# The first eight input-weight blocks loaded as float32 and cast on the chip, in a pooling and retention layer

## What is computed

```python
hn = rms_norm(h, norm_w)                 # norm_w scales the 1024 columns of hn
proj = hn @ w_in                         # w_in: 1024 x 6144 float32
u, gp, q, k, v, gr = split(proj, 6)      # 1024 columns each
pool_o = (trailing means of u over 2/4/8/16 - u) @ w_pool * pool_scale
q, k = rotary(q), rotary(k)
o = retention(q, k, v)                   # chunks of 128 rows, a state per head
ret = rms_norm(o) * ret_norm_w * silu(gr)
y = rms_norm(h + concat(pool_o * silu(gp), ret) @ w_out) * final_norm_w
```

## Time and profile before

| | us |
|---|---|
| median of 3 runs | 619.95 (616.08 to 620.24) |
| the profiled execution | 618.45 |
| its span, slowest core (5) | 616.9 |
| spans of the eight cores | 605.4 to 616.9 |
| PE busy | 570.6 (93%) |
| DVE busy | 414.6 (67%) |
| ACT busy | 266.0 (43%) |
| POOL busy | 112.5 (18%) |

### The profile page before, as it was taken

The page is one execution under the profiler, slowest core; times in us unless marked ns, Lnnn a source line. Parts: engine busy times, 40 slices in busy tenths (PEclk is TensorE's granted clock), DMA queues, the critical chain, the costliest instruction groups (busy, mean ns, idle before and its releaser), DMA issues.

```text
span 616.9 us, 13819 instructions; the slowest of 8 cores (605.4 to 616.9 us)
## 1 busy us (share of the span) xinstructions
PE 570.6 (93%) x4360; PEld 313.9 (51%) x4360; DVE 414.6 (67%) x1114; ACT 266.0 (43%) x831; POOL 112.5 (18%) x131
## 2 busy tenths in 40 slices
PE   0699995999699999999999999999999999899994
PEld 0244452588354646555565646464454655455651
DVE  3349997477888755856676785867767673866463
ACT  2345463553333443343345344353644534355331
POOL 6300001121010111110011122322413310330010
PEclk9999997999899999999999999999999999999998
DMA  8999999486723542544263355575775635454621
GB/s 139 212 168 181 168 172 165 83 112 113 129 73 108 133 126 60 117 103 108 72 114 120 49 171 131 182 159 118 209 137 177 166 102 142 101 152 88 123 69 38
DMA packets 90034, 78.52 MB, mean 127 GB/s; under 512 B 56254, under 2 KB 72814, under 8 KB 89948
## 3 DMA queue, kind: packets, MB, share of 16 engines
q1 hardware_dynamic: 74524, 60.09, 39.5%
q0 software_dynamic: 15440, 17.55, 20.3%
HBM read 64.57 MB, written 18.41 MB: 135 GB/s over the span
## 4 chain that ended last, share of the span: by engine, by line
PE 82%; DMA 9%; DVE 3%; POOL 2%; issue 1%; another core or an unknown queue 1%; SPq 0%; DVEq 0%; POOLq 0%; ACT 0%; ACTq 0%
PE pp L588 42%; PE pp L863 20%; PE pp L603 8%; DMA w_in_bf<-w_in 6%; PE pp L837 2%; DMA w_out_bf<-w_out 2%; PE pp L929 2%; PE pp L916 1%; PE pp L818 1%; PE pp L748 1%; PE pp L707 1%; PE pp L724 1%; PE pp L750 1%; DVE w_in_bf L507 1%
## 5 line engine op out<-in xcount | busy, mean ns | idle before, releaser
L588 PE MATMUL pp<-w_in_bf,hnTs 128*128 128x512 bf16 x1120 | 260.9, 384 | 19.7 <-DMA w_in_bf<-w_in 18.2
L588 PEld LDWEIGHTS pp<-w_in_bf,hnTs 128*128 128x128 bf16 x1120 | 105.4, 99 | 144.3 <-issue 32.5
L863 PE MATMUL pp<-w_out_bf,yT 128*128 128x512 bf16 x448 | 102.2, 383 | 0.3
L623 ACT ACTIVATE F<-pp,dec 128x128 f32<-128x128 f32 (+1 forms) x216 | 61.7, 369 | 59.2 <-PE pp L588 54.1
L863 PEld LDWEIGHTS pp<-w_out_bf,yT 128*128 128x128 bf16 x448 | 43.1, 99 | 53.2 <-issue 4.0
L526 POOL TENSOR_TENSOR rs_r<-rs_r,nh 128x4 f32<-128x4 f32 x32 | 35.5, 1111 | 169.9 <-DVE rs_r L523 169.6
L603 PE MATMUL pp<-hnTs,w_in_bf 128*128 128x128 bf16 x896 | 53.5, 219 | 0.0
L603 PEld LDWEIGHTS pp<-hnTs,w_in_bf 128*128 128x128 bf16 x896 | 51.0, 98 | 3.4 <-issue 0.9
L872 ACT ACTIVATE pp<-xr 128x512 f32<-128x512 f32 x30 | 18.0, 601 | 74.5 <-DVE xr L870 64.5
L910 POOL TENSOR_TENSOR scr<-vM,ident 16x512 bf16<-16x512 bf16 x32 | 35.3, 1102 | 79.4 <-PE pp L916 76.0
L786 DVE SCALAR_TENSOR_TENSOR ry<-pp,rs_r,G 128x128 bf16<-128x128 f32 x104 | 29.2, 343 | 19.6 <-POOL rs_r L526 19.3
(11 more groups left out here) (167 smaller groups left out, 767.0 us busy)
## 6 DMA issues: line engine op xcount, KB each, us to landing
w_in_bf<-w_in POOLq DMA_DIRECT2D x12, 1024.0 KB, 54.8
scr<-S_in SPq DMA_DIRECT2D x32, 256.0 KB, 3.5
Ss<-scr SPq DMA_DIRECT2D x32, 256.0 KB, 3.1
xr<-x SPq DMA_DIRECT2D x15, 512.0 KB, 3.8
y<-xr SPq DMA_DIRECT2D x15, 512.0 KB, 2.8
xA<-x SPq DMA_DIRECT2D x14, 512.0 KB, 4.4
w_out_bf<-w_out POOLq DMA_DIRECT2D x4, 1024.0 KB, 15.2
w_out_bf<-x SPq DMA_DIRECT2D x3, 512.0 KB, 7.4
```

The costliest lines, as they stand in the source:

```text
L588: r = e.matmul(bk(b)[:T, :], lhsT=h.ap[:, kc * T:(kc + 1) * T], rhs=w_in_bf[:, kc, c0:c0 + 512], start=(kc == 0), stop=(kc == 7))
L623: r = e.activation(out=Fa.ap[:T, i * 128:(i + 1) * 128], in_=bk(b)[:T, i * 128:(i + 1) * 128], func=AF.Copy, scale=dec[:T, dslot * 8 + h:d ...
L863: r = e.matmul(bk(b)[:T, :], lhsT=yap[:, kc * st:kc * st + T], rhs=w_out_bf[:, kc, nt * 512:(nt + 1) * 512], start=(kc == 0), stop=(kc == 15))
```

## The change

The first eight blocks no longer go through a casting DMA. SP loads them as float32 into the places of blocks 0 and 1 (loads 0, 2, 4 and 6) and 2 and 3 (loads 1, 3, 5 and 7), which together hold just one float32 block each. DVE, ACT and POOL then each cast a part of the eight 512-column rows of a block (3, 3 and 2) to bf16 in its own place and multiply it by the norm weight in the same operation. The first load is cut in two halves of 1 MB. Blocks 0 to 3 come last, as before by casting DMAs from POOL, when the eight are cast; DVE and ACT fold the norm weight into them, four rows each. So the turned tiles need no factor: A2 copies them out of PSUM with one ACT operation instead of eight on DVE, and `fold_w` is gone. The small loads at the start are put in line with the weight loads on SP's queue "w"; the loads of mask, band, ident and w_out stay on POOL, in a queue "p".

```diff
-WORD = [(10, 11, 6, 7), (8, 9, 4, 5), (2, 3, 0, 1)]
+WORD = (10, 11, 6, 7, 8, 9, 4, 5)
+WLATE = (0, 1, 2, 3)
+SHARE = (("dve", 3), ("act", 3), ("pool", 2))
...
-    def load_w(blk):
+    def wk(blk):
+        return ["win%d%s" % (blk, z) for z in ("dve", "act", "pool", "dvey", "acty", "pooly")]
+
+    def load_w(i, blk):
+        a = i % 2
+        st = w_in_bf[:, :, a * 1024:(a + 1) * 1024].bitcast(F32)
+        parts = 1 if i else 2
+        n = 8 // parts
+        for h in range(parts):
+            sk = [k + "xy"[z] for k in ("st%d" % a,) for z in ((0, 1) if parts == 1 else (h,))]
+            own = wk(2 * a) + wk(2 * a + 1) if i else []
+            ks = slice(h * n, (h + 1) * n)
+            dma("sp", st[:, ks, :], w_in_v[:, ks, blk * 512:(blk + 1) * 512], [], sk + own, (1 << 21) // parts,
+                "d_st%d%d" % (a, h), queue="w")
+            k0 = h * n
+            for z, (eng, m) in enumerate(SHARE if parts == 1 else (("dve", 2), ("act", 1), ("pool", 1))):
+                def f(e, eng=eng, k0=k0, m=m):
+                    r = None
+                    for kc in range(k0, k0 + m):
+                        w = w_in_bf[:, kc, blk * 512:(blk + 1) * 512]
+                        s = normw[:, kc:kc + 1]
+                        if eng == "act":
+                            r = e.activation(out=w, in_=st[:, kc, :], func=AF.Copy, scale=s)
+                        else:
+                            r = e.tensor_scalar(out=w, in0=st[:, kc, :], scalar1=s, scalar2=None, op0=ALU.mult)
+                    return r
...
+    def load_w_late(blk):
         dma("pool", w_in_bf[:, :, blk * 512:(blk + 1) * 512], w_in_v[:, :, blk * 512:(blk + 1) * 512],
-            [], ["win%d" % blk], 1 << 21, queue="w")
+            [], wk(blk) + ["st%d%s" % (blk // 2, z) for z in "xy"], 1 << 21, queue="p")
+        for eng, (k0, k1) in (("dve", (0, 4)), ("act", (4, 8))):
...
-        def ev(e):
-            r = None
-            for kc in range(8):
-                r = e.tensor_scalar(out=d.ap[:, kc * T:(kc + 1) * T], in0=bkb(b)[:, kc * T:(kc + 1) * T],
-                                    scalar1=normw[:, kc:kc + 1], scalar2=None, op0=ALU.mult)
-            return r
-        P.op("dve", ev, reads=[b, "normw"], writes=d.k, cost=c_dve(8, T))
+        act_ev(d.ap, d.k, lambda: bkb(b)[:, 0:8 * T], [b], 8 * T)
...
-    load_x(2, stage[2], stage[1].k)
-    load_x(3, stage[3], stage[2].k)
+    load_w(0, WORD[0])
+    load_x(2, stage[2], queue="w")
+    load_w(1, WORD[1])
+    load_x(3, stage[3], queue="w")
...
+    for i in range(2, 8):
+        load_w(i, WORD[i])
+        if i < 5:
+            load_cs(i, queue="w")
+    for blk in WLATE:
+        load_w_late(blk)
...
-    for ws in WORD:
-        for blk in ws:
-            fold_w(blk)
     fold_w_out()
```

More of the change, by code:

```diff
@@ new lines, in load_w_late, with f @@
+    def load_w_late(blk):
+        dma("pool", w_in_bf[:, :, blk * 512:(blk + 1) * 512], w_in_v[:, :, blk * 512:(blk + 1) * 512],
+            [], wk(blk) + ["st%d%s" % (blk // 2, z) for z in "xy"], 1 << 21, queue="p")
+        for eng, (k0, k1) in (("dve", (0, 4)), ("act", (4, 8))):
+            def f(e, eng=eng, k0=k0, k1=k1):
+                r = None
+                for kc in range(k0, k1):
+                    w = w_in_bf[:, kc, blk * 512:(blk + 1) * 512]
+                    s = normw[:, kc:kc + 1]
+                    if eng == "act":
+                        r = e.activation(out=w, in_=w, func=AF.Copy, scale=s)
+                    else:
+                        r = e.tensor_scalar(out=w, in0=w, scalar1=s, scalar2=None, op0=ALU.mult)
+                return r
+            k = [wk(blk)[("dve", "act", "pool").index(eng)]]
+            P.op(eng, f, reads=["normw"] + k, writes=k,
+                 cost=1.1 if eng == "dve" else c_act(4, 512, ptr=1))
@@ L498, in load_w_out @@
     def load_w_out(b):
         dma("pool", w_out_bf[:, b * 4:(b + 1) * 4, :], w_out_v[:, b * 4:(b + 1) * 4, :],
-            [], ["wo%d%s" % (i, z) for i in range(4 * b, 4 * b + 4) for z in ("", "b")], 1 << 21, queue="w")
-    def fold_w(blk):
-        def f(e):
-            r = None
-            for kc in range(8):
-                w = w_in_bf[:, kc, blk * 512:(blk + 1) * 512]
-                r = e.tensor_scalar(out=w, in0=w, scalar1=normw[:, kc:kc + 1], scalar2=None, op0=ALU.mult)
-            return r
-        P.op("dve", f, reads=["normw", "win%d" % blk], writes=["win%d" % blk], cost=c_dve(8, 512, 4))
+            [], ["wo%d%s" % (i, z) for i in range(4 * b, 4 * b + 4) for z in ("", "b")], 1 << 21, queue="p")
@@ L590, in mm @@
             return r
[L591 removed]
+        P.op("pe", mm, reads=h.k + wk(c0 // 512), writes=[b], cost=c_pe(8, 512))
         return b
@@ L1014, in build_program @@
     order0 = (1, 0, 2, 3, 4)
[L1015 to L1022, removed]
+    dma("pool", mask[:], c_mask[:, :], [], ["mask"], 1 << 16, queue="p")
+    dma("pool", band[:], c_band[:, :], [], ["band"], 1 << 18, queue="p")
+    for i in range(2, 8):
[4 more added lines that the diff above has]
+        load_w_late(blk)
     dma("sp", scr[:, :].bitcast(F32).rearrange("p (g cc d) -> p g cc d", g=4, cc=2),
-        w_pool.rearrange("g (cc p) d -> p g cc d", p=128), ["win4"], sc(0, 8).k, 1 << 20, queue="late")
-    dma("sp", yT_t[:].bitcast(F32), pool_scale[0:1, :].broadcast_to([128, D]), ["win4"], yTk, 1 << 19, queue="late")
-    dma("sp", finw_b[:], finw[0:1, :].broadcast_to([128, D]), ["win1"], ["finw_b"], 1 << 19, queue="late")
+        w_pool.rearrange("g (cc p) d -> p g cc d", p=128), ["win1act"], sc(0, 8).k, 1 << 20, queue="late")
+    dma("sp", yT_t[:].bitcast(F32), pool_scale[0:1, :].broadcast_to([128, D]), ["win1act"], yTk, 1 << 19, queue="late")
+    dma("sp", finw_b[:], finw[0:1, :].broadcast_to([128, D]), ["win3act"], ["finw_b"], 1 << 19, queue="late")
     for i, t in enumerate(order0):
```

32 lines of the change are left out of this document (16 added, 16 removed).

## The result

The changed kernel is slower: 623.73 us (621.1 to 627.46, 20 runs) against 619.69 (616.08 to 623.52, 20 runs), ratio 1.0069 with a 95% interval of 1.0048 to 1.0090. Forecast were 602.5. The spans of the profiled execution are 609.5 to 623.7 us, mean 616.4 over the cores, where before had a mean of 611.0. All rows of the changed kernel here are of core 0, its slowest.

The account below looks back on a forecast made before the run. Loads were taken to set the end only at the start and at 97.5, with PE otherwise mostly full. Terms -8.4 - 3.5 - 4.1 - 1.5 = -17.5 took 618.45 to 601.0 profiled, 602.5 us median; range 590 to 616.

Parts of the forecast that it names:

- so 96.1 + 0.9 + 1.0 + 19.2 = 117.2 for tile 3's inner product: Third late block's landing, fourth's issue, POOL's root and DVE's queue put tile 3's inner product at 117.2, before at 125.64.
- The -8.4: Term for the late blocks: tile 3's inner product on PE comes at 117.2 instead of 125.64.
- Rate: Weight loads in the head: plain float32 loads taken at 0.31 MB/us, little above the 0.30 of casting loads.
- The rival in which the loads are no faster: Loads in the head run at 0.247 MB/us, third late block lands at 118: 623, median 624.5; chance 0.07.
- Start: First block lands at 12.1, first product at 13.5 instead of 19.6; the 6 us count only if no later load is late.
- Order on PE: 32 matmuls of 128 columns and 8 of 512 more ahead of tile 3's inner product fill PE's waiting: -3.5 us.
- The stall behind the weights: At 160.4, PE's wait for DVE's mask falls from 4.98 to 0.9, -4.1, and the slow stretch after it goes, -1.5.
- Casts at nothing: Casts on DVE and POOL and turned copies on ACT cost nothing, since they lie ahead of a PE that is full.
- the sign that the prediction set for shared ports: POOL casts of 2 us would show the rival that DVE and POOL hold each other up: 610, chance 0.18.
- The ring as a throttle: Rival: float32 loads wait for casts of the block two before; at 11 us cast delay 628, slower; chance 0.08.
- behind 175 us the change alters nothing: Claim that the kernel after 175 us stays as it was, the rest of the 616.9 us being full.

Follow-up runs that it names:

- e17: e3 with its order held on every engine and the two waits put back (second late issue for first landing, fourth for third's): 1.0024 to the kernel before.
- e3: Changed kernel with casts on DVE and ACT only (four rows each) and a place key for every late block, so two landing waits go; replanned: 0.9866 to before.
- e6: Changed kernel without any float32 block: twelve casting DMAs, each folded by DVE and ACT as it lands: 0.9927 to the kernel before.
- e16: e3 with its order held, except that casts are again shared 3, 3 and 2 with POOL: 0.9870 to the kernel before.
- e14: Changed kernel's order held, late waits gone, POOL's casts shrunk, fourth late issue ahead of the root, w_pool's fold behind the gated products: 1.0024 to before.
- e15: As e14, with POOL's casts kept: 1.0023 to the kernel before.
- e4: e3 with every float32 block loaded and cast in two halves of 1 MB, four loads in flight: 0.9930 to the kernel before.
- e9: Changed kernel's order held; POOL's part of each cast shrunk to 8 of 512 columns, the rest to DVE and ACT: 1.0044 to the kernel before.
- e10: Changed kernel's order held; only the waits of the second and fourth late issue for a landing removed: 1.0023 to the kernel before.
- e5: Changed kernel with only the first block as float32, the other eleven by casting DMA, folded by DVE and ACT on landing: 0.9943 to the kernel before.

## Why the prediction was wrong, step by step

**The step that failed** is "so 96.1 + 0.9 + 1.0 + 19.2 = 117.2 for tile 3's inner product". It charged 0.9 for the fourth late block, its issue, and 2.1 for the folds of the last two, and nothing for its landing. But the rows of DVE's new order show a fold that waits for `s_d_u15` ahead of that mask, and on ACT a fold of the same block stands ahead of tile 2's squares. ACT's was the one that bound. The load was issued at 104.55 and landed at 118.6, 14 us later; ACT's fold ran from 118.65, DVE stood for the squares behind it (its timeline), and the mask's product came at 133.76:

```profile
122.34 0.17 DVE L560 TENSOR_SCALAR rs_r<-ss_r 128x4 f32<-128x4 f32 x1 [2.33 <-ACT ry L807]
```

From the third block's landing to that product it took 29.7 us (133.76 less 104.02) where the sum has 0.9 + 1.0 + 19.2 = 21.1. The third block itself landed at 104.0 instead of 96.1, and that is a matter of size: 3.3 us lie in the landing of the first block (15.4 for 12.1), 3.9 in the rate from there to the first late block, which was alone in flight for most of its 11.66 us, and 0.7 from its landing to the third's. The -8.4 became +8.1 (133.76 less 125.64, of two different cores; 8.8 in the mean of the eight). e17 measures the two waits at about 10 us in an order that is otherwise good.

*Rate.* 0.31 was too high. In the ring it was 0.28, and e3 to e6 put the last block at 102 to 109 whatever was tried. The rival in which the loads are no faster came nearest, 624.5 as a median, but by luck: it put the third block at 118, where it landed at 104, and it charged nothing for the fourth's landing either.

*Start.* The 6 us, which the sum left out, were 1.0 over the cores. The second half of the first block took 11.55 us from its issue at 3.87 and landed at 15.4, forecast 12.1, and POOL's cast took 1.8. e6 shows that it hardly matters: with a start 7 us later it was faster than before.

*Order on PE.* The work is there: on every core 32 matmuls of 128 columns and 8 of 512 more stand ahead of tile 3's inner product, and PE is busy 3.9 us longer up to it (mean of the cores). But it did not fill a wait; PE stands 6.0 us longer there all the same.

*The stall behind the weights.* Right: 4.98 to 0.92, forecast 0.9, and 8.38 to 6.91; in the mean of the cores 3.8 to 0.5. That it came out to a tenth is luck: from the issue of w_out's third part to PE's start it took 15.95 us instead of 18.1 (149.66 to 165.61), and PE had 15.03 us of work in it instead of 17.2. e6, without float32 loads, has part of this gain (1.0 in the mean, but 2.7 on its slowest core).

*Casts at nothing.* Right for the end, by e16 and by e14 against e15. The durations were wrong (see below), and the sign that the prediction set for shared ports, POOL casts of 2 us, did show without the cost: 6 of the 16 took over 2.0. The ring as a throttle is refuted by e4.

*Not in the sum.* w_pool and pool_scale, asked for 33 us later; and "behind 175 us the change alters nothing" failed, by PE's wait for a residual row at 193, 2.8 us in the mean. It belongs to the order: it stands on seven or eight cores of each of e9 to e15, which keep that order, while in the kernel before and in the runs with other orders no core stands over 0.8 us for such a row up to 250. What in the order puts that load late I did not follow further.

**Still open** is what in the planner's order for e3 is worth the rest, about 1.6 per cent between it and e14. The residual row (3.4 us in e14) can be a part of it; for the others, single rows were moved twice, and each move uncovered the next wait.

## What to carry to other kernels

When a load gets a wait, follow it to the last instruction that needs its bytes, on every in-order engine, and charge issue plus landing, not issue alone. Two loads that share a name in a dependence table but no bytes are one behind the other for nothing; in e3's order that cost 10 us, while in the changed kernel's own order taking the waits away (e10) gained less than could be told from the noise. And an edit that feeds a planner is two edits: hold the order to measure the one, and hold the work to measure the other.

## What the runs showed of the hardware that I had not expected

A POOL operation that casts 128x512 from float32 to bf16 takes 1.8 us in the middle and 1.56 at least, not the 1.03 of the 16x512 row that I took it from in the earlier trace rows:

```profile
L520 DVE TENSOR_SCALAR w_in_bf<-w_in_bf,normw x25: 466/486/916, 12.6 to 76.2; 128x512 bf16<-128x512 f32 x25
L520 POOL TENSOR_SCALAR w_in_bf<-w_in_bf,normw x16: 1559/1808/3570, 12.7 to 76.0; 128x512 bf16<-128x512 f32 x16
```

Both engines have a tail: POOL up to 3.57, DVE 0.92 where it mostly takes 0.49. The two POOL casts during which DVE did nothing (at 26.32 and 37.17) took 1.56 each, and in e3, where POOL casts nothing, DVE's tail is gone:

```profile
L520 DVE TENSOR_SCALAR w_in_bf<-w_in_bf,normw x32: 470/481/487, 13.6 to 74.5; 128x512 bf16<-128x512 f32 x32
```

So each engine holds the other up. The Trainium skill (SBUF — State Buffer, Who interferes with whom) says that DVE in a two-port mode and GpSimd exclude each other for a whole instruction, and these tails agree with it in kind. In e16, which is as fast as e3, they are much the same:

```profile
L520 DVE TENSOR_SCALAR w_in_bf<-w_in_bf,normw x25: 470/486/917, 13.7 to 76.7; 128x512 bf16<-128x512 f32 x25
L520 POOL TENSOR_SCALAR w_in_bf<-w_in_bf,normw x16: 1559/1940/3420, 13.9 to 77.6; 128x512 bf16<-128x512 f32 x16
```

So the contention is there, and in a good order it cost nothing that could be measured.

The load rate of eight cores that read the same 25 MB was much the same for casting and for plain loads, in blocks of 2 MB or 1 MB, two or four in flight or all at once: the twelfth block was there at 102 to 109 us in e3, e4, e5 and e6, and at 106 to 112 before. What bounds it was not measured by itself.
